# Where the last transposes of an mLSTM head go, and where the output projection begins

## The reference, cut to what matters

```
s = einsum('bthd,bshd->btsh', q, k) * exp(dmat - m_t)
num = einsum('btsh,bshe->bthe', s, v) + w_inter * einsum('bhed,bthd->bthe', c_st, q)
h = num / maximum(abs(den), exp(-m_t))
c_new = w_c * c_st + einsum('bsh,bshe,bshd->bhed', w_s, v, k)
...
h = h * rsqrt(mean(h * h) + EPS) * norm_g
y = (h * o_gate) @ w_out
```

## Time and profile before

| | us |
|---|---|
| median of three runs | 2940.21 |
| the profiled execution's own time | 2939.81 |
| its span | 2938.0 |
| TensorE busy | 2823.3 (96%) |
| DVE, POOL, ScalarE busy | 1068.2, 807.7, 539.9 |
| granted TensorE clock, mean | 0.98 |
| end of the three looped heads' position 8 (first matmul of unit 10) | 1526.77, 1688.05, 1851.15 |
| first matmul of the output projection | 1992.07 |

### The profile page before, as it was taken

One profiled execution on the slowest core, in us unless ns is written; L12 is line 12 of the kernel. 1 busy time (PEld: TensorE's weight loads), 2 busy tenths in 40 slices (PEclk: granted clock), 3 DMA queues, 4 the chain that ended last, 5 costly groups with the idle time before them and its releaser, 6 DMA issues.

```text
span 2938.0 us, 39826 instructions
## 1 busy us (share of the span) xinstructions
PE 2823.3 (96%) x15943; PEld 2723.9 (93%) x15943; DVE 1068.2 (36%) x1476; ACT 539.9 (18%) x937; POOL 807.7 (27%) x576
## 2 busy tenths in 40 slices
PE   7999989999999999998999999999999999999995
PEld 7997769999999999998989898979999999999995
DVE  5127844322222222256545454552522222222225
ACT  3113631100010011031312213141201100100011
POOL 6542002222232222222121211342222222222221
PEclk9999979999999999999999999999999999999997
DMA  6321021111111111122132231432111111111111
GB/s 184 70 57 30 0 76 41 44 43 43 36 43 43 43 43 43 43 101 59 31 93 31 73 66 51 81 113 97 44 43 36 43 43 36 50 43 36 42 44 65
DMA packets 106515, 161.59 MB, mean 55 GB/s; under 512 B 55496, under 2 KB 66760, under 8 KB 105656
## 3 DMA queue, kind: packets, MB, share of 16 engines
q1 hardware_dynamic: 32368, 100.72, 12.2%
q10 hardware_dynamic: 73784, 58.55, 6.9%
q0 software_dynamic: 272, 0.98, 0.1%
HBM read 130.45 MB, written 24.47 MB: 53 GB/s over the span
## 4 chain that ended last, share of the span: by engine, by line
PE 82%; issue 10%; DVE 4%; POOL 2%; ACT 1%; DMA 0%; ACTq 0%; DVEq 0%; POOLq 0%
PE psum L562 73%; PE psum L653 2%; PE psum L776 1%; PE psum L589 1%; POOL w_lo L436 1%; DVE h_lo L1049 1%; DVE mid L1046 1%; PE psum L734 1%; ACT mid L1540 1%; PE psum L752 1%; POOL mid L515 1%; POOL w_hi L433 0%; PE psum L874 0%; DVE mid L1016 0%; DVE low L1509 0%
## 5 line engine op out<-in xcount | busy, mean ns | idle before, releaser
L433 POOL TENSOR_SCALAR w_hi<-w_raw 128x1024 fp32r<-128x1024 f32 x191 | 204.4, 1070 | 1774.5 <-PE psum L562 1564.7
L562 PE MATMUL psum<-a_hi,w_hi 128*128 128x384 f32 x2808 | 655.1, 341 | 37.1 <-DVE a_lo L1004 16.0
L562 PE MATMUL psum<-a_lo,w_hi 128*128 128x384 f32 x2808 | 642.6, 336 | 0.0
L562 PE MATMUL psum<-a_hi,w_lo 128*128 128x384 f32 x2808 | 641.6, 336 | 0.0
L562 PEld LDWEIGHTS psum<-a_hi,w_hi 128*128 128x128 f32 x2808 | 502.1, 190 | 46.0 <-issue 24.1
L562 PEld LDWEIGHTS psum<-a_lo,w_hi 128*128 128x128 f32 x2808 | 504.8, 189 | 0.0
L562 PEld LDWEIGHTS psum<-a_hi,w_lo 128*128 128x128 f32 x2808 | 504.4, 189 | 0.0
L436 POOL TENSOR_TENSOR w_lo<-w_raw,w_hi 128x1024 fp32r<-128x1024 f32 x191 | 460.8, 2412 | 15.9
L1038 DVE TENSOR_TENSOR low<-psum,low 128x1152 f32<-128x1152 f32 x144 | 195.5, 1357 | 646.0 <-PE psum L562 645.9
L562 PE MATMUL psum<-h_hi,w_hi 128*128 128x384 f32 x1536 | 350.4, 335 | 7.9 <-DVE h_lo L1049 7.9
L562 PE MATMUL psum<-h_lo,w_hi 128*128 128x384 f32 x1536 | 348.8, 334 | 0.0
(11 more groups left out here) (219 smaller groups left out, 2362.7 us busy)
## 6 DMA issues: line engine op xcount, KB each, us to landing
w_raw<-in_wall SPq DMA_DIRECT2D x191, 512.0 KB, 3.6
low<-in_x ACTq DMA_DIRECT2D x16, 576.0 KB, 9.1
high<-in_mem_in ACTq DMA_DIRECT2D x32, 257.0 KB, 3.8
out_mem_s<-high ACTq DMA_DIRECT2D x32, 257.0 KB, 3.1
out_x_spill<-low ACTq DMA_DIRECT2D x8, 576.0 KB, 2.7
low<-out_x_spill ACTq DMA_DIRECT2D x8, 576.0 KB, 9.4
out_y<-low ACTq DMA_DIRECT2D x8, 576.0 KB, 2.9
out_mix_spill<-mid ACTq DMA_DIRECT2D x3, 1152.0 KB, 5.3
```

The costliest lines, as they stand in the source:

```text
L433: nc.gpsimd.tensor_scalar(w_hi[:, s, :], w_raw[:, s, :], 1.0, 1.0, ALU.mult, ALU.mult)\
L562: r = mm(psum[:, z + i, 0:TN], w[:, s, k * P:(k + 1) * P], a[:, kk, tok(i)], start=first and n == 0, stop=last and n == 2)
```

## The change

The transposes of positions 7 and 8 get places outside banks 2 and 3 (`hidden_place`): bank 7 (`STREAM_BANK`) for position 7 and bank 6 (`PIECE_BANK`) for position 8. `gate_out` on DVE reads them there. Those of position 7 wait for less. Those of position 8 move into the next unit, ahead of its fifth block k = 4: unit 10 in the looped heads, unit 0 of the output projection in the last, which thereby begins inside the last head. Ahead of that unit TensorE waits for the last readers of banks 3, 4 and 5, and ahead of unit 11 for the last `gate_out`. The table `BACK_SPLITS` says behind which position POOL splits which block of `back`.

```diff
+BACK_SPLITS = {3: (0,), 4: (1, 2), 5: (3,), 6: (4,), 7: (5,)}
...
+        def hidden_place(p, k):
+            if p < NLC - 1:
+                return psum[:, 2 + k, HT:HT + P]
+            bank = STREAM_BANK if p == NLC - 1 else PIECE_BANK
+            return psum[:, bank, P * k:P * (k + 1)]
...
-                    if last and p > LAST_O:
-                        k = p - LAST_O - 1
+                    for k in BACK_SPLITS.get(p, ()) if last else ():
...
                 def hidden_back(p):
                     pe.wait_ge(hn_done, 9 * h + (p + 1))
-                    if p >= 1:
-                        pe.wait_ge(mix_done, 9 * h + (p + ONE))
-                    pe.wait_ge(num_done, 9 * h + min(p + 2, NLC + 1))
-                    pe.wait_ge(tb_done, 9 * h + min(p + 2, NLC + 1))
+                    if p < NLC - 1:
+                        if p >= 1:
+                            pe.wait_ge(mix_done, 9 * h + (p + ONE))
+                        pe.wait_ge(num_done, 9 * h + (p + 2))
+                        pe.wait_ge(tb_done, 9 * h + (p + 2))
+                    elif p == NLC - 1:
+                        pe.wait_ge(tb_done, 9 * h + NLC)
+                    elif not last:
+                        pe.wait_ge(evicted, 8 * h + (B_HEAD + 10))
...
-                hidden_back(NLC)
-                if not last:
-                    pe.wait_ge(mix_done, 9 * h + (9 + ONE))
-                    pe.wait_ge(csu_done, 8 * h + (8 + ONE))
+                pe.wait_ge(tb_done, 9 * h + 9)
+                pe.wait_ge(cu_done, 9 * h + 9)
+                pe.wait_ge(csu_done, 8 * h + (8 + ONE))
+                def tail(k):
+                    if last:
+                        heads_split(k)
+                    if k == 4:
+                        pe.wait_ge(mix_done, 9 * h + (8 + ONE))
+                        hidden_back(NLC)
+                if last:
+                    unit(U_OUT1 % 2, U_OUT1 + 1, B_OUT1, B_OUT1 - 1, tail)
+                else:
                     for j in (10, 11):
...
+                        if j == 11:
+                            pe.wait_ge(mix_done, 9 * h + (9 + ONE))
...
-            for j in range(8):
+            for j in range(1, 8):
...
-                        r = V.scalar_tensor_tensor(out=mix[:, k, q], in0=psum[:, 2 + k, HT:HT + P],
+                        r = V.scalar_tensor_tensor(out=mix[:, k, q], in0=hidden_place(p, k),
```

More of the change, by code:

```diff
@@ L824, in _, with heads_split @@
             pe.wait_ge(aux_read, AX_R3)
+            def heads_split(k):
+                if k < KT - 2:
+                    pe.wait_ge(back_split, k + 1)
+                else:
+                    pe.wait_ge(lo_done, 3 * KT + (k - KT + 3))
             def head(h, last):
@@ L923, in hidden_back @@
                     pe.wait_ge(hn_done, 9 * h + (p + 1))
-                    if p >= 1:
-                        pe.wait_ge(mix_done, 9 * h + (p + ONE))
-                    pe.wait_ge(num_done, 9 * h + min(p + 2, NLC + 1))
-                    pe.wait_ge(tb_done, 9 * h + min(p + 2, NLC + 1))
+                    if p < NLC - 1:
[7 more added lines that the diff above has]
+                        pe.wait_ge(evicted, 8 * h + (B_HEAD + 10))
                     for k in range(2):
-                        r = tr(psum[:, 2 + k, HT:HT + P], hn[:, p % 2, P * k:P * k + P], ident)
+                        r = tr(hidden_place(p, k), hn[:, p % 2, P * k:P * k + P], ident)
                     r.then_inc(ht_done, 1)
@@ L962, in head @@
                         hidden_back(p - 1)
-                hidden_back(NLC)
-                if not last:
-                    pe.wait_ge(mix_done, 9 * h + (9 + ONE))
-                    pe.wait_ge(csu_done, 8 * h + (8 + ONE))
+                pe.wait_ge(tb_done, 9 * h + 9)
[9 more added lines that the diff above has]
+                    unit(U_OUT1 % 2, U_OUT1 + 1, B_OUT1, B_OUT1 - 1, tail)
+                else:
                     for j in (10, 11):
                         b = B_HEAD + j
-                        unit((U_HEAD + j) % 2, 8 * h + (U_HEAD + j + 1), b, 8 * h + (b - 1))
+                        if j == 11:
+                            pe.wait_ge(mix_done, 9 * h + (9 + ONE))
+                        unit((U_HEAD + j) % 2, 8 * h + (U_HEAD + j + 1), b, 8 * h + (b - 1), tail if j == 10 else None)
             with pe.Fori(0, MH - 1) as h:
@@ L973, in _ @@
             head(MH - 1, True)
[L976 to L982, removed]
-            for j in range(8):
+            for j in range(1, 8):
                 u, b = U_OUT1 + j, B_OUT1 + j
-                unit(u % 2, u + 1, b, b - 1, heads_split if j == 0 else None, last_use=j == 7)
+                unit(u % 2, u + 1, b, b - 1, last_use=j == 7)
             ff(U_FF1, B_FF1, 3 * KT + 2, (AX_R3, 3))
```

## The result

The changed kernel took 2918.93 us in the median of six runs (2914.46 to 2925.19), the one before 2939.24 us in six on the same chip (2935.01 to 2942.7). The ratio is 0.993, 95% interval [0.992, 0.994]: faster by 20.3 us, where 13.4 were forecast. The sign was right and each place named did gain; the size was too small.

A forecast was written before the change was run, and what follows sets the result against it. TensorE was taken to bound the kernel, at 82% of the chain that ends last. Looped heads 7.6, clock 1.6 and last head 4.2 sum to 13.4 us, from 2939.8 to 2926.4 us, range 2922.5 to 2932.5.

The forecast's parts named there:

- What bounds the kernel: Whole kernel: 82% of the chain that ends last is TensorE, so a microsecond counts only if TensorE idles or runs slower.
- The looped heads: Ends of the three looped heads: 3.10 us before unit 10 shrink to two transpose pairs, gaining 2.54 us each, 7.6 together.
- The clock behind one tail: Second looped head: with the hole gone the granted clock no longer falls behind it, 1.6 us back.
- Unit 12 and the history: Looped heads: history lands near 1539.5 instead of 1534.5, but TensorE needs DVE's eviction only at unit 12; cost nothing.
- The double pair: Last head: POOL's two pairs of splits behind position 4 make position 6's numerator chain end 2.85 us late.
- the matmuls L954 of position 8 ended at 1983.35 + 1.92 = 1985.27; now 1988.1: Last head: position 8's matmuls end at 1988.1, so unit 0 starts at 1989.05 instead of 1992.07.
- the first rival: Last head: a new 2.1 us hole lowers the clock, leaving a gain of 10.3 us, 2929.5 us; chance 0.22.
- Unit 0: Output projection's first unit: lasts 13.1 us where it took 14.32, ending at 2002.15, 4.2 us earlier.
- Lock-outs at every position: Last head, positions 5 to 7: shifted pairs shut out DVE, 7.9 us of gain go, 2934.3 us; chance 0.07.
- the late history: Looped heads: history landing after 1549 makes unit 12 wait; at 6.5 us per head, 2946 us; chance 0.03.
- the double pair costs nothing: Last head: something else set position 5's pace, so 2.85 us more are gained, 2923.5 us; chance 0.05.

The follow-up runs named there:

- e2_last_only: The last head as changed, the three looped heads with the old places and waits of the kernel before; 2935.95 us (ratio 0.998 to the kernel before).
- e9_before_unrolled: The kernel before with TensorE's queue of the three looped heads written out instead of looped; 2928.5 us (ratio 0.9969).
- e10_after_unrolled: The changed kernel with TensorE's queue of the three looped heads written out instead of looped; 2916.4 us (ratio 0.9927 to the kernel before).
- e12_change_again: The changed kernel once more, unedited; 2920.03 us (ratio 0.9943 to the kernel before).
- e1_looped_only: The three looped heads as changed, the last head with the old places, waits and split table; 2929.26 us (ratio 0.9956 to the kernel before).
- e6_pair_ahead: The changed kernel with position 7's splits doubled instead of position 4's, and position 8's transposes ahead of the next unit; 2932.63 us (0.9976 to the kernel before).
- e8_splits_behind: The changed kernel with all six pairs of POOL's splits of `back` behind position 8 of the last head; one run of 2934.18 us.

## Why the prediction was right and wrong

- **What bounds the kernel: right.** The gains that the profiles show lie where TensorE had idled or run at 1.2 GHz.
- **The looped heads: right, slightly small.** 2.54 us per head were forecast, 2.73 measured. The second pair costs the 0.25 that stood in the sum; the first costs 0.25 too, and not the 0.31 of rows 4, whose distance has waits in it. The other 0.1 is a term that the 3.10 did not hold: behind its wait the old unit 10 also started slowly, 1.66 us for its first three groups (1526.77 to this row of the kernel before) where 1.56 is their rhythm.

```profile
1528.43 0.68 PE L562 MATMUL psum<-a_hi,w_hi 128*128 128x384 f32 x3
```

- **The clock behind one tail: right.** 1.6 forecast; head 1 gave 4.31 - 2.73 = 1.58. That it was this one head is chance: the old tail brought a fall in every program that has it, but in changing heads: head 1 before, heads 1 and 2 in `e2_last_only`, heads 0 and 1 in `e9_before_unrolled`.
- **Unit 12 and the history: right.** The eviction became late (DVE idled 5.94 us for the history) and nothing waited for it.
- **The double pair: right by mechanism and size.** A hole of 2.1 us forecast, 1.99 measured; L1454 (L1434 before) shut out for 1.35 us; position 6's transposes later by 2.65 us where 2.85 were forecast. The Trainium skill, SBUF — State Buffer, section on who interferes with whom, calls the port pair that DVE and GpSimd share an exclusive lock held for a whole instruction; by that rule, the trace agrees (L1454 ends with L533).
- **The step that failed: "the matmuls L954 of position 8 ended at 1983.35 + 1.92 = 1985.27; now 1988.1".** That carried the old half clock of position 8 over into the new schedule without a reason. It ran at full clock: unit 0 began 5.72 us earlier measured from position 4's transposes (25.68 before, 19.96 after), not 3.02. Of the 2.7 between, 2.46 are the way from position 6's transposes to the end of the update (6.07 us before, 3.61 after), 0.20 the smaller delay and the rest the start of unit 0. I had priced the clock once as a gain (unit 0) and once as a risk (the first rival), and never as a gain between the two. The rival saw that the new hole would lower it, which it did (0.66 over 1956 to 1960), but not that position 8 could be free of it. Why position 8 kept its clock is open: `e10_after_unrolled` and `e12_change_again` repeat it, but the same last head lost it in `e2_last_only`, and the old one kept it in `e1_looped_only`. So part of these 2.46 us may be luck.
- **Unit 0: right.** 13.1 us forecast, 13.27 measured, with one wait at k = 6 that costs about 0.4 us where 0.25 stood.
- **What the sum did not hold.** The edges of the loop, 3.1 us, and the attention stretch, 4.0 us, in the profiled executions. Terms: 13.4 forecast; the changed stretches gave 16.5 (0.6 more from the tails, 2.6 from the last head); the other 3.8 of the 20.3 lie in untouched code, whose clock differs from profile to profile. With 16.5 alone the time would have been 2922.7 us, just inside the range; a range built only from the touched stretches was too narrow for the rest.

Of the rivals, none came out. Lock-outs at every position and the late history are refuted by the rows above; "the double pair costs nothing" holds net to within 1.2 us, by another road than the one named. The rival of the clock had the fall right and the time wrong.

## What to carry to other kernels

A short result of the last step can be moved into the middle of the next long stream of matmuls, if it gets a bank of its own: here two pairs of transposes that stood in a 3.1 us hole then cost 0.50 us. When idle time moves, price the clock anew in every stretch behind it, at both levels, and count what a wait covers. And before a change of half a per cent is read, compare the untouched stretches of both profiles first, and look which execution of its set each profile took; they moved by 7 us here, and two profiles that agree can both come from the short end of their sets.

## What was not expected of the hardware

- TensorE's hand-written queue idles where its loop branches back, 2.65 to 3.54 us in the kernels before and after and 2.13 to 4.12 in the looped experiments, with the lower clock behind it in some cases (1.32 us for a group at 1547.91, 0.79 at 1705.65). Written out, the idle time is gone; the kernel before gained 10.0 us at two edges.
- Which hole lowers the clock is not told by its length. The old tail (1.43 and 0.89 us idle) lowered it in one looped head of three in one program and in two of three in two others; the 1.50 us of `e6_pair_ahead` in none. In the last head a hole of 1.48 us did in `e8_splits_behind`, and the 2.49 us of `e1_looped_only` did not.
- A pair of 128x128 transposes in a stream of matmuls costs 0.25 us. The Trainium skill, TensorE: Matmul & The Clock Gate, Part 4, has about 275 ns for one in a kernel's context; an estimate from that figure, with no overlap, gives 1.1 us for the two pairs of a tail. The trace has less than half of it: 0.50.
